# One matmul per block and head in the levels of a gated linear recurrence, with keys gathered by GpSimd

## What is computed

```
def gla_scan(q, k, v, log_f, s0):
    ...
    def step(s, blk):
        qc, kc, vc, gc = blk
        b = jnp.cumsum(gc, axis=2)
        diff = b[:, :, :, None, :] - b[:, :, None, :, :]
        decay = jnp.where(lower, jnp.exp(jnp.where(lower, diff, 0.0)), 0.0)
        scores = jnp.einsum('bhtd,bhsd,bhtsd->bhts', qc, kc, decay)
        o = scores @ vc + jnp.einsum('bhtd,bhde->bhte', qc * jnp.exp(b), s)
        ...

def bidir_scan(q, i, fwd, bwd, s_fwd, s_bwd):
    o_f, sf_out = gla_scan(q, fwd[0], i, fwd[1], s_fwd)
    o_b, sb_out = gla_scan(flip(q), flip(bwd[0]), flip(i), flip(bwd[1]), s_bwd)
    return o_f + flip(o_b), sf_out, sb_out
```

## Time and profile before

| | |
|---|---|
| median of 3 runs | 1813.0 us (1812.96 to 1814.63) |
| span of the profiled execution | 1812.9 us |
| TensorE busy | 1737.4 us, 96% |
| TensorE weight loads busy | 1286.0 us, 71% |
| VectorE busy | 851.8 us, 47% |
| ScalarE busy | 687.6 us, 38% |
| GpSimd busy | 4.2 us, 6 instructions |
| moved by DMA | 480.46 MB, mean 265 GB/s |

### The profile page before, as it was taken

The page is one execution under the profiler, slowest core; times in us unless marked ns, Lnnn a source line. Parts: engine busy times, 40 slices in busy tenths (PEclk is TensorE's granted clock), DMA queues, the critical chain, the costliest instruction groups (busy, mean ns, idle before and its releaser), DMA issues.

```text
span 1812.9 us, 28102 instructions
## 1 busy us (share of the span) xinstructions
PE 1737.4 (96%) x11446; PEld 1286.0 (71%) x11446; DVE 851.8 (47%) x1206; ACT 687.6 (38%) x897; POOL 4.2 (0%) x6
## 2 busy tenths in 40 slices
PE   6999999999999999999899999999999999998988
PEld 3677677888887799989777877766536887763343
DVE  2435425434533656767569876554105555410001
ACT  4332622222224646445477755443004444400001
POOL 0000000000000000000000000000000000000000
PEclk9999999999999999999999999999999999999999
DMA  9835266433632221321169999999999999999997
GB/s 349 310 139 184 87 218 234 160 93 132 240 95 69 93 87 54 94 90 40 70 264 393 351 342 409 409 409 409 409 409 409 408 407 408 404 408 409 409 409 289
DMA packets 161986, 480.46 MB, mean 265 GB/s; under 512 B 14992, under 2 KB 58176, under 8 KB 155712
## 3 DMA queue, kind: packets, MB, share of 16 engines
q1 hardware_dynamic: 161856, 478.66, 69.5%
HBM read 477.56 MB, written 1.05 MB: 264 GB/s over the span
## 4 chain that ended last, share of the span: by engine, by line
PE 74%; DMA 12%; SPq 6%; DVE 4%; ACT 2%; issue 2%; DVEq 0%; ACTq 0%
PE ps L754 18%; PE ps L756 17%; PE ps L755 17%; SPq L701 5%; PE ps L1533 5%; DMA arena<-in_moe_up 3%; PE ps L1604 3%; DMA raw<-in_moe_up 3%; DVE w_lo L2076 2%; DMA arena<-in_moe_w 2%; PE ps L773 1%; PE ps L1522 1%; PE ps L1167 1%; PE ps L1165 1%; PE ps L1596 1%
## 5 line engine op out<-in xcount | busy, mean ns | idle before, releaser
L2076 DVE TENSOR_TENSOR w_lo<-raw,w_hi 128x1024 fp32r<-128x1024 f32 x220 | 264.8, 1221 | 268.6 <-ACT w_hi L1687 266.2
L1687 ACT ACTIVATE w_hi<-raw 128x1024 fp32r<-128x1024 f32 x220 | 229.4, 1056 | 377.6 <-PE ps L756 307.9
L754 PE MATMUL ps<-h_hi,w_hi 128*128 128x512 f32 (+1 forms) x736 | 279.2, 379 | 3.3 <-DVE h_lo L2158 2.2
L756 PE MATMUL ps<-h_lo,w_hi 128*128 128x512 f32 (+1 forms) x736 | 273.3, 371 | 0.0
L755 PE MATMUL ps<-h_hi,w_lo 128*128 128x512 f32 (+1 forms) x736 | 273.0, 371 | 0.0
L2076 DVE TENSOR_TENSOR w_lo<-arena,w_hi 128x1024 fp32r<-128x1024 f32 x114 | 137.0, 1222 | 76.9 <-ACT w_hi L1687 73.2
L754 PEld LDWEIGHTS ps<-h_hi,w_hi 128*128 128x128 f32 x736 | 138.6, 188 | 47.6 <-issue 21.5
L756 PEld LDWEIGHTS ps<-h_lo,w_hi 128*128 128x128 f32 x736 | 138.6, 188 | 24.7
L755 PEld LDWEIGHTS ps<-h_hi,w_lo 128*128 128x128 f32 x736 | 138.8, 189 | 22.6 <-issue 0.5
L1687 ACT ACTIVATE w_hi<-arena 128x1024 fp32r<-128x1024 f32 x114 | 119.3, 1059 | 93.4 <-DMA arena<-in_moe_up 45.6
L754 PE MATMUL ps<-w_hi,s_hi 128*128 128x512 f32 x336 | 135.0, 402 | 4.8 <-DVE w_lo L2076 4.7
(11 more groups left out here) (387 smaller groups left out, 2541.5 us busy)
## 6 DMA issues: line engine op xcount, KB each, us to landing
arena<-in_moe_up SPq DMA_DIRECT2D x188, 512.0 KB, 14.6
raw<-in_moe_up SPq DMA_DIRECT2D x156, 512.0 KB, 14.8
a_slots<-in_moe_up SPq DMA_DIRECT2D x104, 512.0 KB, 14.9
arena<-in_moe_w SPq DMA_DIRECT2D x98, 512.0 KB, 15.0
raw<-in_moe_w SPq DMA_DIRECT2D x78, 512.0 KB, 15.1
arena<-in_w_ada SPq DMA_DIRECT2D x35, 1024.0 KB, 5.0
raw<-in_ffn_w SPq DMA_DIRECT2D x66, 512.0 KB, 5.8
a_slots<-in_moe_w SPq DMA_DIRECT2D x48, 512.0 KB, 15.1
```

Source lines behind the costliest of these rows:

```text
L754: pe.matmul(dst, s_h, m_h, start=start, stop=False, **kw)
L756: return pe.matmul(dst, s_h, m_l, start=False, stop=stop, **kw)
L1687: act.activation(w_hi[:, o % R, :], src, ACT.Copy).then_inc(hi_done, 1)
L2076: dve.tensor_tensor(w_lo[:, o % R, :], src, w_hi[:, o % R, :].bitcast(F32), ALU.subtract).then_inc(lo_done, 1)
```

## The change

A level is now one matmul per segment and head with 128 moving columns (L1166 in the new file): its queries are, in the order of the tokens, each block's near half from the backward queries and far half from the forward queries (`woven`), read in place. To have the fitting keys in one stationary operand, GpSimd gathers them into a tile of its own, `keys`: of each block the near half from the forward keys and the far half from the backward ones. For level 0 it copies all 512 elements once the gates are done (k_rdy). For a later level it copies the inner quarters of each block, which the widening doesn't touch, as soon as the level before has let go of `keys` (l_mm), and the outer quarters behind the widening (l_wide), and then lets TensorE go (k_cp). Products of keys and queries of the same half come out as well; the mask leaves them out. The forward and backward queries change places in the arena, and one tile is laid out elsewhere to make room for `keys`.

```
+R_TB, R_TF = R_T, R_T + G_LAT
...
+        keys = sb("keys", [P, G_LAT])
...
+        def woven(a, b, hs, w):
+            both = arena[:, a:a + 2 * (b - a)].rearrange("p (s x) -> p s x", s=2)[:, :, 0:G_LAT]
+            return both.rearrange("p s (b c) -> p b s c", c=2 * hs)[:, :, :, 0:w]
...
             def level(g, n):
                 b, hs = base(g), LEVELS[n]
+                pe.wait_ge(k_cp, len(LEVELS) * g + n + 1)
...
-                        pe.matmul(far(dst, hs), ar(b + R_KF + at, P), far(ar(b + R_T + at, P), hs),
-                                  start=True, stop=True, skip_group_check=True)
-                        m = pe.matmul(near(dst, hs), ar(b + R_KB + at, P), near(ar(b + R_T + G_LAT + at, P), hs),
+                        m = pe.matmul(ps[:, 6 - n % 2, (seg * HG + h) * P:(seg * HG + h + 1) * P],
+                                      keys[:, at:at + P], woven(b + R_TB + at, b + R_TF + at + hs, hs, hs)[:, 0:P // (2 * hs)],
                                       start=True, stop=True, skip_group_check=True)
...
+            def level_keys(g, n):
+                b, hs = base(g), LEVELS[n]
+                if n == 0:
+                    if g > 0:
+                        pool.wait_ge(l_mm, len(LEVELS) * g)
+                    pool.wait_ge(k_rdy, 2 * g + 2)
+                    pool.tensor_copy(keys.rearrange("p (b s c) -> p b s c", s=2, c=hs),
+                                     woven(b + R_KF, b + R_KB + hs, hs, hs)).then_inc(k_cp, 1)
+                    return
+                w = hs // 2
+                quarters = keys.rearrange("p (b q c) -> p b q c", q=4, c=w)
+                pool.wait_ge(l_mm, len(LEVELS) * g + n)
+                pool.tensor_copy(quarters[:, :, 1:3], woven(b + R_KF + w, b + R_KB + hs, hs, w))
+                pool.wait_ge(l_wide, len(LEVELS) * g + n)
+                pool.tensor_copy(quarters[:, :, 0::3], woven(b + R_KF, b + R_KB + hs + w, hs, w)).then_inc(k_cp, 1)
+
+            for g in range(NG):
+                for n in range(len(LEVELS)):
+                    level_keys(g, n)
...
-                for at, (x, y) in ((R_LF, (R_KF, R_T + hs)), (R_LB, (R_T + G_LAT, R_KB + hs))):
+                for at, (x, y) in ((R_LF, (R_KF, R_TF + hs)), (R_LB, (R_TB, R_KB + hs))):
```

More of the change, by code:

```diff
@@ L281, in build @@
         h_lo = sb("h_lo", [P, KT * NT], F32R)
-        s_hi = sb("s_hi", [P, 3072 - A_SIDE], F32R)
-        s_lo = sb("s_lo", [P, 3072 - A_SIDE], F32R)
         arena = sb("arena", [P, ARENA])
@@ L319, in build @@
         with nc.sbuf_tensor("a_parts", [P, 2, A_SIDE], F32R) as a_parts:
-            pass
+            with nc.sbuf_tensor("s_parts", [P, 2, 3072 - A_SIDE], F32R) as s_parts:
+                pass
         a_slots = sb("a_slots", [P, 2 * A_SIDE // UNIT, UNIT])
+        keys = sb("keys", [P, G_LAT])
+        s_hi, s_lo = s_parts[:, 0, :], s_parts[:, 1, :]
         ps = es.enter_context(nc.psum_tensor("ps", [P, 8, BANK], F32))
@@ L389, in build @@
         b_rdy, l_wide, l_upd, l_mm, l_cp = sem("b_rdy"), sem("l_wide"), sem("l_upd"), sem("l_mm"), sem("l_cp")
+        k_cp = sem("k_cp")
         i_mul, o_mm, o_sq, o_sum = sem("i_mul"), sem("o_mm"), sem("o_sq"), sem("o_sum")
@@ L539, in halves @@
             return both.rearrange("p s (b c) -> p s b c", c=2 * hs)[:, :, :, 0:hs]
-        def near(view, hs):
-            return view.rearrange("p (b c) -> p b c", c=2 * hs)[:, :, 0:hs]
-        def far(view, hs):
-            return view.rearrange("p (b c) -> p b c", c=2 * hs)[:, :, hs:]
+        def woven(a, b, hs, w):
+            both = arena[:, a:a + 2 * (b - a)].rearrange("p (s x) -> p s x", s=2)[:, :, 0:G_LAT]
+            return both.rearrange("p s (b c) -> p b s c", c=2 * hs)[:, :, :, 0:w]
         def by_half(bank):
@@ L1163, in level @@
                         at = h * N_LAT + seg * P
-                        dst = ps[:, 6 - n % 2, (seg * HG + h) * P:(seg * HG + h + 1) * P]
-                        pe.matmul(far(dst, hs), ar(b + R_KF + at, P), far(ar(b + R_T + at, P), hs),
-                                  start=True, stop=True, skip_group_check=True)
-                        m = pe.matmul(near(dst, hs), ar(b + R_KB + at, P), near(ar(b + R_T + G_LAT + at, P), hs),
+                        m = pe.matmul(ps[:, 6 - n % 2, (seg * HG + h) * P:(seg * HG + h + 1) * P],
+                                      keys[:, at:at + P], woven(b + R_TB + at, b + R_TF + at + hs, hs, hs)[:, 0:P // (2 * hs)],
                                       start=True, stop=True, skip_group_check=True)
@@ L1201, in outputs @@
                     pe.matmul(dst, ar(b + R_V + HG * P + h * P, P), s1[:, h, :], start=False, stop=False)
-                    pe.matmul(dst, ar(b + R_KF + G_LAT + h * P, P), lat(b + R_T)[:, h, :], start=False, stop=False)
-                    m = pe.matmul(dst, ar(b + R_KB + G_LAT + h * P, P), ctx(b + R_T)[:, h, :], start=False, stop=True)
+                    pe.matmul(dst, ar(b + R_KF + G_LAT + h * P, P), lat(b + R_TF)[:, h, :], start=False, stop=False)
+                    m = pe.matmul(dst, ar(b + R_KB + G_LAT + h * P, P), lat(b + R_TB)[:, h, :], start=False, stop=True)
                 m.then_inc(o_mm, 1)
@@ L1240, in cross @@
                 b = base(g)
-                for d, (keys, queries) in enumerate(((lat(b + R_KF), lat(b + R_T)), (lat(b + R_KB), ctx(b + R_T)))):
+                for d, (keys, queries) in enumerate(((lat(b + R_KF), lat(b + R_TF)), (lat(b + R_KB), lat(b + R_TB)))):
                     s, t = slice(d * P, (d + 1) * P), slice((1 - d) * P, (2 - d) * P)
@@ L2382, in queries @@
                 for d in range(2):
-                    m = dve.tensor_tensor(o_part(g, d), ar(base(g) + R_Q, G_LAT),
+                    m = dve.tensor_tensor(ar(base(g) + (R_TF, R_TB)[d], G_LAT), ar(base(g) + R_Q, G_LAT),
                                           ar(base(g) + (R_LF, R_LB)[d], G_LAT), ALU.mult)
@@ L2409, in widen_last @@
                 b = base(g)
-                for at, t, (to, by) in ((R_LF, lat(b + R_T), (1, 0)), (R_LB, ctx(b + R_T), (0, 1))):
+                for at, t, (to, by) in ((R_LF, lat(b + R_TF), (1, 0)), (R_LB, lat(b + R_TB), (0, 1))):
                     v = t[:, :, to * P:(to + 1) * P]
```

## The result

| | before | changed |
|---|---|---|
| median | 1813.8 us (1813.0 to 1816.0, 4 runs) | 1803.8 us (1802.4 to 1804.5, 4 runs) |
| span of the profiled execution | 1812.9 us | 1801.6 us |
| TensorE busy | 1737.4 us | 1722.0 us |
| VectorE busy | 851.8 us | 865.3 us |
| GpSimd busy | 4.2 us | 45.1 us |

The changed kernel takes 0.994 of the time before (95% interval 0.9927 to 0.9954). It is faster by 10 us in the medians and by 11.3 us in the spans; 17.3 us were forecast, for 1795.6 us. The time lies at the upper end of the range, 1789 to 1804 us.

What follows compares the result with a forecast made beforehand. TensorE was taken to bound the levels of the first three head pairs, weight traffic the stage from 1200 us. Saving 22.6 us less copy costs of 5.3 us gave 17.3 us: 1812.9 to 1795.6 us, range 1789 to 1804 us.

Steps and rivals of the forecast that it cites:

- Rival A: Level 0 gets no cheaper, as its alternating moving columns are fetched slower: 3.5 us less saved, 1799.1 us; chance 0.13.
- (a): Between pairs 0 and 1, and 1 and 2: GpSimd copies hold VectorE up on the path, 2.4 us (0 to 5.0).
- (b): Path of pair 2 from 827.92 us on: two copies hold VectorE up, 0.6 us (0 to 1.3).
- (c): Pair 3, level 3 to level 6: six copies hold VectorE up, 1.8 us (0 to 3.8).
- (d): Last level of pair 3 must wait for a copy instead of VectorE's totals: 0.5 us (0.2 to 0.8).
- rival C: A half copy has a large fixed cost, eating the gain from 1.2 us each; at 1.5 us, 1822.8 us; chance 0.06.
- rival D: Woven columns pass at half speed at every level; TensorE saves nothing, costs stay: 1816.5 us; chance 0.04.
- Rival B: TensorE idles longer at 836 us and within levels 3 to 6, its clock falls: 5 us lost, 1800.6 us; chance 0.11.

Runs made afterwards that it cites:

- the dummy matmuls: Changed kernel with four dummy matmuls of 512 bf16 columns on TensorE between the last cross product and the last outputs: 1802.4 us, 0.9932 of before.
- the seven and five profiles above: Last norm's memset to end: seven profiles of the changed kernel and variants without 32-byte pad, 913.9 to 916.2 us; kernel before and four padded profiles, 912.7 to 913.0.
- the pad: Unused tile of 32 bytes ahead of a_parts: changed kernel 1799.6 us, 0.9916 of before; kernel before with it 1812.7 us, 0.9989.
- the moved cross copy: Changed kernel with the last pair's cross copy on ScalarE put ahead of the split of the second expert unit: 1799.5 us, 0.9913 of before.
- two keys tiles: Changed kernel with two keys tiles in turn, the next level's front copy right behind this level's back copy: 1802.3 us, 0.9933 of before.

## Why the prediction was right, and where it was not

**What bounds the kernel**: right. At the end of the last level 16.5 us stood of the 17.3 forecast. One part was too simple: the stage of the experts was called bound by weight traffic, but TensorE is busy 475 of 500 us there, and matmuls slower by 7 ns cost 2.0 us, so it binds in places.

**What is saved**: 22.6 us forecast, 21.3 measured. From start to start a level saves 0.47 us (level 0), 0.75 (level 1) and 0.90 (levels 2 to 6), 5.7 us a pair instead of 6.1. So pairs 0 and 1 gave 11.4 us for 12.2; pair 2's levels 0 to 5 gave 42.02 - 37.14 = 4.9 for 5.2; pair 3's levels 0 to 3 give 0.47 + 0.75 + 2 x 0.90 = 3.0 for 3.5; level 6 took 1.48 us in place of 3.44, 2.0 for 1.7. Level 6 of pair 3 is not a fixed number: for the clock it took 3.44, 3.43 and 2.14 us in the profiles of the kernel before and its variants, 0.9 to 1.7 in those of the changed one. Rival A was half right: level 0 costs 0.37 us more, not 0.87, but level 1 lost 0.15 of its saving too, about half of it by its runs of two. That fetch rule as I read it in SBUF - State Buffer of the Trainium skill (Door 1: The DMA port swizzle) would have spared level 1; the measurement decides.

**The costs on VectorE**: right in kind, close in size. (a) 2.4 us forecast; 1.24 + 1.36 = 2.6 measured, as level 6 to outputs took 0.34 and 0.46 us more instead of 0.90 less. The hold-up by a whole copy was 0.60, as taken; by a half copy 0.22 to 0.25 for 0.3. The wait itself, some 1.2 us for L2437, is in the trace with 1.09 and 1.19. (b) 0.6 forecast, 0.47 measured. (c) and (d) 2.3 together; 1.2 by the kernel without half copies. TensorE's waits for the back copy in pair 3, levels 4 to 6:

```profile
851.24 1.13 PE L1166 MATMUL ps<-arena,keys 128*128 128x128 f32 x8 [0.42 <-POOL keys L1686]
856.36 1.13 PE L1166 MATMUL ps<-arena,keys 128*128 128x128 f32 x8 [1.15 <-POOL keys L1686]
...
860.68 1.84 PE L1166 MATMUL ps<-arena,keys 128*128 128x128 f32 x8 [3.18 <-POOL keys L1686]
```

They look like 4.8 us lost to GpSimd and are 1.2: without half copies TensorE stands 0.81 and 2.77 us at levels 5 and 6 all the same. The copies took 0.41 to 0.95 us for the 0.5 and 1.0 assumed; rival C had no chance, and rival D, half speed at every level, is gone with the 0.81 us.

At the last level's end the forecast's sum stood at 17.3 and the trace at 16.5 us. That they are so close is luck in part: 1.3 us less was saved than forecast, and 1.0 us less was paid.

**What failed** is the step from there to the end, one sentence in the prediction: "So a microsecond won before that norm is won at the end." It rested on SyncE's wait for h_lo and on VectorE's and TensorE's rows; ScalarE's queue between level 6 and the outputs was not looked at. There the cross copy stood behind the split of an expert weight whose DMA comes 9 us after TensorE's levels. The 1.9 us of level 6, which the prediction counted as bare, were hidden by it. That was visible before: two places ahead of the cross copy (L1890) ScalarE waited 4.36 us for a weight's DMA, and TensorE stood 2.07 us ahead of the outputs.

```profile
885.87 1.06 ACT L1687 ACTIVATE w_hi<-raw 128x1024 fp32r<-128x1024 f32 x1 [4.36 <-DMA raw<-in_moe_up]
887.12 1.06 ACT L1687 ACTIVATE w_hi<-raw 128x1024 fp32r<-128x1024 f32 x1 [0.19 <-DMA raw<-in_moe_up]
888.08 0.64 ACT L1890 ACTIVATE arena<-ps 128x256 f32<-128x256 f32 x2
...
888.82 0.67 PE L1200 MATMUL ps<-arena 128*128 128x256 f32 x2 [2.07 <-issue]
```

**Rival B, the clock**, came at other places than named. At 823.6 us, in the path of pair 2, TensorE had stood 2.35 us and the cross product took nearly twice its time, hidden behind ScalarE's gate_exp, which ran from 821.09 to 826.10:

```profile
823.64 2.08 PE L1244 MATMUL ps<-arena 128*128 128x128 f32 x8 [2.35 <-DVE arena L2426]
```

What it cost was 1.7 us at the outputs of pair 3, in the execution profiled first and not in the second; the dummy matmuls took it away in the trace.

**What no rival had** is the placement of a tile. The diff moves s_hi and s_lo into s_parts, and the prediction passed over that as costless. It cost 2.0 us in the stage of the experts, by the seven and five profiles above. Ahead of the first level 144 more matmuls read these tiles at 6 to 7 ns more, by this estimate 0.9 us; of the 0.4 us lost there in the first profile it may be the cause. That the slower matmuls come from the 32 bytes is shown, by what path inside the chip is not.

So the measured time lies in the range, but not for the reason that the range was given: its upper end, 1804 us, stood for rivals A and B, and what filled it was the cross copy, the clock at the outputs and the placement.

Taken together for the first profile: 21.3 saved, 4.3 to the copies on the path, 0.4 before the first level and 0.1 in small pieces, make the 16.5; 1.9, 1.7 and 1.6 behind them leave 11.3 us. With the pad, the moved cross copy and two keys tiles the kernel takes 1795.5 us, the number of the forecast, but this is a coincidence and no proof of it, since the first two edits bring most of their gain to the kernel before as well: like against like, the change is worth 12.9 to 14.2 us, not 17.3.

## What to carry to other kernels

After the last place that a change speeds up, follow the gain through every queue to the end, in-order copies behind a DMA above all; a stage with one engine waiting for weights swallows microseconds that all the others hand on. When a tile is laid out anew, compare its start with the old one, modulo 64 and 128 bytes, and the distance between the starts of the matmuls that read it. A fix that wins time behind a change must be given to the kernel before as well, or its gain is booked to the change. A wait that a trace puts down to a new helper is its cost only as far as leaving it out shortens the path.

## What the runs showed of the hardware

- The 512-column matmuls on tiles that begin 32 bytes past a multiple of 64 bytes (96 past one of 128) took 394 to 396 ns at the median, and 389 ns at a multiple of 128, whether the tile was the moving operand or the weights; between two starts 232 to 235 and 227 ns.
- 128 moving fp32 columns that alternate element by element between two rows took 1.18 us for eight instructions, with runs of two elements 0.97, with longer runs or contiguous ones 0.81, or 0.89 where an fp32 matmul follows as it does behind the runs of two.
- A GpSimd copy of 256 elements in runs of 16 or 32 goes from 0.40 to 0.93 us beside VectorE's pair of instructions with two SBUF inputs and holds the pair up by 0.21 us, in single elements by 0.47 us; a memset of the same elements, 0.31 to 0.33 us, doesn't hold it up and isn't stretched.
- Ahead of the same matmuls the clock fell from 2.4 to 1.2 GHz after 3.1 to 4.3 us of idleness in five profiles and didn't after 3.5 and 3.75 in two others; at other places it fell after 1.91 and 2.35 us. What an idle stretch of that length costs can't be read from one execution.
